# Weights ahead of tokens, statistics in pairs: a reordered start of a two-layer diffusion kernel

## The reference, cut to what matters

```python
shift, scale, gate = silu(c) @ ada_w[0] + ada_b[0]            # for latent tokens
c_shift, c_scale, c_gate = silu(c_ctx) @ ada_w[0] + ada_b[0]  # for context tokens
hx = rmsnorm(x, norm_w[0]) * (1 + scale) + shift
hc = rmsnorm(ctx, norm_w[0]) * (1 + c_scale) + c_shift
lb = softmax-cumsum of the lower-bound logits                 # tables for the gates
f  = lb + (1 - lb) * sigmoid(h @ w_f)                         # forward and backward gates
v, q, z = h @ w_v, silu(h @ w_q), silu(h @ w_z)
```

## Time and profile before

| what | value |
|---|---|
| median of 3 runs | 2157.39 us (2153.93 to 2157.52) |
| the profiled execution | 2153.69 us, with a span of 2151.9 us |
| TensorE busy | 2059.3 us, 96% |
| VectorE busy | 1304.1 us, 61% |
| ScalarE busy | 931.9 us, 43% |
| GpSimd busy | 476.2 us, 22% |
| moved by DMA | 144.45 MB, 67 GB/s over the span |

### The profile page before, as it was taken

The page is one execution under the profiler, slowest core; times in us unless marked ns, Lnnn a source line. Parts: engine busy times, 40 slices in busy tenths (PEclk is TensorE's granted clock), DMA queues, the critical chain, the costliest instruction groups (busy, mean ns, idle before and its releaser), DMA issues.

```text
span 2151.9 us, 30236 instructions
## 1 busy us (share of the span) xinstructions
PE 2059.3 (96%) x11372; PEld 1490.5 (69%) x11554; DVE 1304.1 (61%) x2360; ACT 931.9 (43%) x1960; POOL 476.2 (22%) x450
## 2 busy tenths in 40 slices
PE   5799999999999999999999999899999999999998
PEld 2567767767767767767767767677766666666665
DVE  7848648648648548548548548755563637465444
ACT  5746346346346346346356356344423131314222
POOL 2032222222222221221221222200161312100000
PEclk8899999999999999999999999999999999999999
DMA  7220110110110110110110110543321111204443
GB/s 278 79 69 11 45 55 11 45 54 11 45 54 11 46 53 11 47 53 11 54 45 11 60 40 1 186 147 122 123 71 50 45 51 33 88 10 148 147 147 117
DMA packets 106753, 144.45 MB, mean 67 GB/s; under 512 B 7136, under 2 KB 74224, under 8 KB 105584
## 3 DMA queue, kind: packets, MB, share of 16 engines
q1 hardware_dynamic: 99648, 125.72, 18.1%
q10 hardware_dynamic: 6960, 16.80, 2.0%
HBM read 108.91 MB, written 33.57 MB: 66 GB/s over the span
## 4 chain that ended last, share of the span: by engine, by line
PE 80%; ACT 7%; DVE 7%; issue 3%; DMA 2%; POOL 0%; SPq 0%; DVEq 0%; ACTq 0%; POOLq 0%
PE bank L1308 22%; PE bank L1309 21%; PE bank L1313 20%; PE bank L1464 4%; PE bank L1443 3%; PE bank L1475 3%; PE bank L1548 3%; PE bank L1450 2%; DVE xb L1074 2%; ACT xa L727 1%; ACT xa L729 1%; PE bank L1427 1%; ACT xb L737 1%; DVE xa L1038 1%; DMA ada_sb<-in_ada_w 1%
## 5 line engine op out<-in xcount | busy, mean ns | idle before, releaser
L1308 PE MATMUL bank<-h_hi,w_hi 128*128 128x512 f32 (+1 forms) x1472 | 576.6, 396 | 0.0
L1309 PE MATMUL bank<-h_hi,w_lo 128*128 128x512 f32 (+1 forms) x1472 | 550.6, 379 | 0.0
L1308 PEld LDWEIGHTS bank<-h_hi,w_hi 128*128 128x128 f32 x1472 | 279.3, 190 | 54.7
L1309 PEld LDWEIGHTS bank<-h_hi,w_lo 128*128 128x128 f32 x1472 | 279.3, 190 | 47.6
L1313 PE MATMUL bank<-h_lo,w_bf 128*128 128x512 bf16 (+1 forms) x1351 | 303.3, 365 | 7.9 <-issue 1.3
L1313 PEld LDWEIGHTS bank<-h_lo,w_bf 128*128 128x128 bf16 x1472 | 133.7, 98 | 142.7 <-issue 25.1
L1117 DVE SCALAR_TENSOR_TENSOR w_st<-w_st,cv,bank 128x128 f32<-128x128 f32 x560 | 194.2, 347 | 24.1 <-DVE w_st L1117 0.5
L1308 PE MATMUL bank<-wo_hi,og_hi 128*128 128x512 f32 x496 | 197.9, 399 | 3.1 <-DVE og_lo L1154 2.2
L1309 PE MATMUL bank<-wo_hi,og_lo 128*128 128x512 f32 x496 | 193.6, 390 | 0.0
L612 POOL TENSOR_TENSOR q<-qp,cv 128x512 f32<-128x512 f32 x64 | 71.9, 1124 | 524.9 <-PE bank L1443 244.1
L586 POOL TENSOR_TENSOR w_hi<-w_raw,zero_col 128x512 fp32r<-128x512 f32 x80 | 91.9, 1149 | 430.7 <-DMA w_raw<-in_w_in 228.7
(11 more groups left out here) (180 smaller groups left out, 3543.8 us busy)
## 6 DMA issues: line engine op xcount, KB each, us to landing
w_raw<-in_w_in SPq DMA_DIRECT2D x80, 256.0 KB, 2.8
ada_sb<-in_ada_w SPq DMA_DIRECT2D x8, 1024.0 KB, 13.9
xt<-in_x SPq DMA_DIRECT2D x16, 512.0 KB, 6.5
ada_a<-in_ada_late SPq DMA_DIRECT2D x64, 128.0 KB, 2.1
ada_b<-in_ada_late SPq DMA_DIRECT2D x64, 128.0 KB, 2.1
gated_scratch<-o_t ACTq DMA_DIRECT2D x32, 256.0 KB, 2.4
xr<-in_x SPq DMA_DIRECT2D x16, 512.0 KB, 5.0
x_scratch<-xr ACTq DMA_DIRECT2D x16, 512.0 KB, 2.6
```

Source lines behind the costliest of these rows:

```text
L1308: pe.matmul(out_ap, hi, m_hi, start=start, stop=False)
L1309: pe.matmul(out_ap, lo, m_hi, start=False, stop=False)
```

## The change

SyncE loads the eight pieces of `ada_w` ahead of the two context tiles. The statistics of the context tiles move behind the rounding of `ada_w`. Latent tiles are handled in pairs by `token_pair`: two sums of squares, then one logarithm and one exponential for both. Tiles 2 and 3 are done before the first modulate; the other pair of the group behind modulate 3 of the context group, and in later groups the pairs come behind modulates 2 and 5. VectorE scales a pair after the split that follows. The gate tables (`head_tables`) are made at step 3, ahead of the split of the last group, and `hv` and `hg` are copied there for head 0. GpSimd waits at step 0 until `hf_ready` is 32 (four groups split) before it cuts halves 2 and 3.

```diff
+        def pair_behind(g, k):
+            if g + 1 == len(GT0):
+                return None
+            return {3: GT0[1][0] + 2}.get(k) if g == 0 else {2: GT0[g + 1][0], 5: GT0[g + 1][0] + 2}.get(k)
+
+        def token_pair(act, t):
+            for i in (t, t + 1):
+                act.wait_ge(s[f"x_in{i % 8}"], 16 * (i // 8 + 1))
+                act.activation(junk0[:, :], xt0[:, i % 8, :], ACT.Square, accum_out=ssq[:, 0, i:i + 1]
+                               ).then_inc(s["nrm_act"], 1)
+                act.wait_ge(s["nrm_act"], 3 * t + i - t + 1)
+            act.activation(rstd[:, 0, t:t + 2], ssq[:, 0, t:t + 2], ACT.Ln, scale=1.0 / D,
+                           bias=eps[:, 0:1]).then_inc(s["nrm_act"], 2)
+            act.wait_ge(s["nrm_act"], 3 * t + 4)
+            act.activation(rstd[:, 0, t:t + 2], rstd[:, 0, t:t + 2], ACT.Exp, scale=-0.5
+                           ).then_inc(s["nrm_act"], 2)
+            rms_n[0] += 6
...
@@ modulate_first, ScalarE
-                if k % 2 and g + 1 < len(GT0):
-                    token_stats(act, GT0[g + 1][0] + k // 2)
+                if pair_behind(g, k) is not None:
+                    token_pair(act, pair_behind(g, k))
...
@@ SyncE
-            for t in range(2):
-                load_x0(sp, t)
             for k in range(KT):
                 sp.dma_start(ada_sb[:, k, :, :], ...)
+            for t in range(2):
+                load_x0(sp, t)
...
@@ GpSimd, head
+                    if first and st == 0:
+                        pool.wait_ge(s["hf_ready"], KT * (len(GT0) - 1))
                     for dh, m in CUTS.get(st, []):
...
@@ ScalarE
-            for t in range(2):
-                token_stats(act, t)
             (rounding of ada_w)
+            token_stats(act, 0)
             (copies of mrow, two exponentials for the tables)
+            token_stats(act, 1)
+            token_pair(act, 2)
             act.wait_ge(s["set_dve"], 5)
             modulate_first(act, 0)
...
@@ VectorE
-            for t in range(2):
-                normalise(t)
             (remainders of ada_w)
+            normalise(0)
             (copies of mrow)
-            (eleven instructions of the gate tables)
+            normalise(1)
             (gadd, gmul)
+            def head_tables():
+                (the same eleven instructions)
...
@@ split_first, VectorE
-                    if k % 2 and g + 1 < len(GT0):
-                        normalise(GT0[g + 1][0] + k // 2)
+                    if k and pair_behind(g, k - 1) is not None:
+                        for t in range(2):
+                            normalise(pair_behind(g, k - 1) + t)
+            for t in range(2, 4):
+                normalise(t)
             split_first(0)
...
@@ head, VectorE
+                if not first:
+                    head_vectors(h)
                 for st in range(NG):
+                    if first and st == NBLK - 1:
+                        head_tables()
+                        head_vectors(h)
                     if first and st < NBLK:
                         split_first(st + 1)
...
-                    if st == 2:
+                    if st == (NBLK - 1 if first else 2):
                         need(dve, "og_ready", NBLK, h, 0)
                         dve.tensor_copy(hg[:, :], head_tab[:, bass.ds(h, 1), 5]).then_inc(s["head_vec"], 1)
```

More of the change, by code:

```diff
@@ L934, in normalise @@
             def normalise(t):
-                dve.wait_ge(s["nrm_act"], 3 * (t + 1))
+                dve.wait_ge(s["nrm_act"], 3 * (t + 1 if t < 2 else t // 2 * 2 + 2))
                 dve.tensor_scalar(xt0[:, t % 8, :], xt0[:, t % 8, :], rstd[:, 0, t:t + 1], None,
                                   ALU.mult).then_inc(s["xn0"], 1)
-            for t in range(2):
-                normalise(t)
             for n in range(2 * KT):
@@ L969, in _ @@
                                          ALU.add, ALU.mult).then_inc(s["set_dve"], 1)
+            def head_tables():
+                dve.wait_ge(s["set_act"], 3)
+                step(dve.tensor_tensor(lbt[:, 4, :], lbt[:, 2, :], lbt[:, 3, :], ALU.add))
+                step(dve.reciprocal(lbt[:, 4, :], lbt[:, 4, :]))
+                step(dve.tensor_tensor(lbt[:, 0, :], lbt[:, 2, :], lbt[:, 4, :], ALU.mult))
+                for d in range(2):
+                    step(dve.tensor_copy(head_tab[:, :, 2 * d], lbt[:, 0, 8 * d:8 * d + 8]))
+                    step(dve.tensor_scalar(head_tab[:, :, 2 * d + 1], lbt[:, 0, 8 * d:8 * d + 8], -1.0, 1.0,
+                                           ALU.mult, ALU.add))
+                    step(dve.tensor_scalar(head_tab[:, :, 6 + d], lbt[:, 0, 8 * d:8 * d + 8], 1.0, None,
+                                           ALU.subtract))
+                step(dve.tensor_copy(head_tab[:, :, 5], vcol[:, R_GN:R_GN + 8]))
+                dve.tensor_copy(late[:, :], vcol[:, R_ADAB + 2 * KT:R_ADAB + 6 * KT]).then_inc(s["late_sum"], 1)
             def split_first(g):
@@ L982, in split_first, with head_vectors @@
                                       ).then_inc(s["hf_ready"], 1)
-                    if k % 2 and g + 1 < len(GT0):
-                        normalise(GT0[g + 1][0] + k // 2)
+                    if k and pair_behind(g, k - 1) is not None:
[3 more added lines that the diff above has]
+                normalise(t)
             split_first(0)
-            def head(h, first, last):
+            def head_vectors(h):
                 dve.tensor_copy(hv[:, :], head_tab[:, bass.ds(h, 1), :].rearrange("p a b -> p (a b)")
@@ L991, in head @@
                 need(dve, "head_vec", 2, h, 1)
+            def head(h, first, last):
+                if not first:
+                    head_vectors(h)
                 for st in range(NG):
+                    if first and st == NBLK - 1:
+                        head_tables()
+                        head_vectors(h)
                     if first and st < NBLK:
```

## The result

| | before | changed |
|---|---|---|
| median of 11 runs each, us | 2155.09 (2152.06 to 2157.91) | 2161.09 (2156.63 to 2163.46) |
| ratio, with its 95% interval | | 1.0025 [1.0016, 1.0034] |
| profiled execution: span, us | 2151.9 | 2160.1 |

The changed kernel is slower by 5.4 us (0.0025 x 2155.09); the interval of the ratio gives 3.4 to 7.3 us, and the two medians differ by 6.0. So the kernel did get slower; the 4.3 us that the prediction took for the least that can be told lie inside this interval. That figure started from 2157.39, a median of three; eleven executions of the kernel before give 2155.09.

A forecast was written before the change was run, and what follows sets the result against it. TensorE, busy from 108 us on in a fixed order, was taken to pass on any shift of the start almost unchanged. Terms -6.1 - 2.0 + 4.9 + 6.7 + 1.9 = +5.4 us on 2157.39 gave 2162.8 us, range 2153 to 2166.

The forecast's parts named there:

- opening: Start to first modulate: weights loaded first and tables off the path bring it to 36.7 from 42.83 us, -6.1 us.
- context group: From its first modulate to group 1's: one pair replaces four single statistics, 10.2 us instead of 12.15, -2.0 us.
- groups 1 to 3: Intervals between first modulates: pairs make ScalarE and VectorE wait in turn, 48.3 us instead of 43.4 for three, +4.9 us.
- tables beside cuts: Step 3, ahead of group 4's split: VectorE's table instructions are stretched by GpSimd's deferred cuts, +6.7 us.
- low clock: Last transposes of group 4: TensorE, idle before, runs at 1.2 GHz, transposes 1.77 us apart, +1.9 us.
- sum at the marker: Shift of the fifth group's last transpose, at 104.59 us before: all terms together, +5.4 us.
- from the marker to the third `k_tok`: Stretch from the fifth group's last transpose into head 0: the shift was to arrive almost unchanged, 0 us added.
- The rival in which ScalarE sets the pace: Groups 1 to 3: intervals shrink by 0.9 us, giving -2.7 instead of +4.9; total 2155.2 us; 16%.
- The rival in which they run side by side: Step 3: tables run beside GpSimd's cuts unstretched, costing 2.4 us, 4.3 less; total 2158.5 us; 14%.
- The rival of full clock: Groups 1 to 4: TensorE stays at full clock, groups cost 2.0 us and the clock nothing; total 2158.0 us; 20%.

The follow-up runs named there:

- cuts at 36: Changed kernel with one-tile statistics in groups 1 to 3, gate tables behind the last split, GpSimd's halves 2 and 3 cut from `hf_ready` 36; ratio to before 0.9964.
- single statistics: Changed kernel with statistics of groups 1 to 3 made one tile at a time behind every second modulate, as before; ratio to the kernel before 0.9988.
- the two experiments: Changed kernel with late tables and undeferred cuts, once with pairs kept (2151.75 us, one execution), once with one-tile statistics in groups 1 to 3 (ratio to before 0.9969).
- Cuts at once: Changed kernel without GpSimd's wait at step 0, so halves 2 and 3 are cut right behind the first slice; tables stay at step 3; 2155.99 us, one execution.
- tables after the split: Changed kernel with gate tables and `hg` moved to step 4, behind the last group's split; GpSimd's cuts stay deferred; 2160.29 us, one execution.
- cuts at 8 and 16: Changed kernel with one-tile statistics in groups 1 to 3, tables behind the last split, half 2 cut at `hf_ready` 8, half 3 at 16; ratio to before 0.9966.
- its best part alone: Changed kernel with one-tile statistics in groups 1 to 3, tables behind the last split, cuts not deferred; ratio to the kernel before 0.9969.

## Why the prediction was right, step by step

| step | predicted | first profiles | second profiles |
|---|---|---|---|
| opening | -6.1 | -7.1 | -5.8 |
| context group | -2.0 | -1.8 | -2.0 |
| groups 1 to 3 | +4.9 | +4.0 | +5.5 |
| tables beside cuts | +6.7 | +6.2 | +6.2 |
| low clock | +1.9 | +1.95 | +1.95 |
| sum at the marker | +5.4 | +3.15 | +5.8 |
| from the marker to the third `k_tok` | 0 | +1.7 | +0.8 |

Each column of profiles compares one execution of the changed kernel with one of the kernel before. The mean at the marker is +4.5, 0.9 below the forecast: the opening brought 0.4 more, and the tables cost 0.5 less. The step of the tables is the first split's distance behind its modulate, 6.96 us against 0.80.

**The opening** was a microsecond larger than I gave it in the first profile, and 0.3 smaller in the second. The mechanism stands: with the context tiles first, the first modulate moves by 4.5 us, and most of what isn't bytes is work that meets GpSimd. But I fixed this term too precisely. The changed kernel's second profile has its first modulate at 36.88, close to my 36.7, and cuts at 36, whose opening has no other edit, at 37.43 against 35.73 in single statistics. In these two TensorE was at a different clock between 32 and 34.5 us, first single statistics, then cuts at 36:

```profile
32.00:34.50 2.50, 2.50 (x20) 2.50 (x19) 0.89 (x1) 2.40 (x7) 2.50 (x3) 0.76 1.04 411
```

```profile
32.00:34.50 2.50, 2.50 (x14) 2.50 (x13) 0.86 (x1) 2.40 (x7) 2.50 (x3) 0.50 1.05 413
```

Where the clock is 0.50, the turning of `mrow` into columns ends later (`gadd` starts at 34.61 in the changed kernel's first profile and at 35.80 in its second), and the rest with it. A term on which an opening's waits and clock bear has a spread of 1 to 2 us.

**The pairs.** That two engines that took turns with overlap now wait for each other was right, and the idle 2.35 us of VectorE under a pair show it. The size was right too. The three intervals took 16.1, 16.0 and 15.3 us in the first profile, the last with the full clock at its start, for which I had 15.2; and 15.5, 16.5 and 16.1 in the second, against my 15.6, 16.3 and 16.3. Over all the runs, three intervals with pairs take 46.3 to 48.1 us (six profiles), and 41.2 to 43.4 with single statistics and no cuts beside them (five, with the two of before). The 3.9 us that the two experiments give lie at the low end of this. The rival in which ScalarE sets the pace is out: intervals would have been under 14.5.

**Tables beside cuts.** Six of twelve instructions ended with one of GpSimd's six, as worked out. "Cuts at once" and "tables after the split" take away one of the two each, and in both the stretch behind group 4's first modulate shrinks (8.64 and 10.74 us, not 14.28). The rival in which they run side by side is out; 2.4 us, its price, is what the tables take alone. The step came out 0.5 us below its 6.7: GpSimd's six took 5.6 us from start to end, where I had 5.9, and with the reciprocal passing only five small instructions were left behind them.

The Trainium skill's rule ("SBUF — State Buffer", sections "Summary: rules for kernel authors" and "Who interferes with whom") holds here: VectorE and GpSimd share a port pair as an exclusive lock, and its list of the VectorE instructions that ask for it has no reciprocal. The trace agrees with both. The reciprocal took 0.25 us at 94.94 beside GpSimd's `w_bf`, and 0.25 alone in "cuts at once".

**The clock.** The size was right to a tenth, and the experiment that keeps the clock up shows it to be the clock and not the pace of VectorE. The rival of full clock is out for the changed kernel. At this step it holds in "single statistics", though, where TensorE waited 2.83 us and not 5.97. The length of the last wait alone doesn't decide it: the clock was 0.50 behind a wait of 1.77 us in "tables after the split" (102 to 106 us), and low behind one of 2.76 in "cuts at once" (0.70 between 94 and 98). So the terms don't add up when one is taken away. Undoing the pairs gave 8.1 us at the marker: 3.9 ahead of group 4's first modulate, 2.3 because the tables were done sooner behind it (4.7 us, not 7.0), and 1.9 of clock.

**What failed** is the sentence that behind the marker TensorE waits for nothing and the shift arrives unchanged. In head 0 it waits for ScalarE's `k_tok`, for 3.2 and 3.1 us in the two profiles of the changed kernel and for 1.5 and 3.1 in those of before, and falls to a low clock in both kernels. From the second to the third copy of `k_tok` it took 8.46 and 8.52 us in the changed kernel, 6.67 and 7.27 in that of before. That the total matched +5.4 to the tenth is luck: the mean at the marker was 0.9 short, 1.3 was added behind it, which the prediction had put at nothing, and the ratio's own interval is 3.4 to 7.3 us. The direction and the terms ahead of the marker are not luck. Whether the 1.3 us belong to the change is open. From the marker to the third `k_tok` the two profiles of before took 68.7 and 69.9 us and the two of the changed kernel 70.5 and 70.7, but "cuts at 8 and 16" and "cuts at 36", which have none of its three costly edits, took 70.2 and 70.9. In the kernel before a stretch at low clock fell at another place:

```profile
153.00:156.00 3.00, 3.00 (x9) 2.35 (x8) 1.92 (x2) 1.77 (x5) 0.00 (x0) 0.51 0.00 0
```

So what arrives of a shift at the start is the shift within one or two microseconds, as these waits and stretches of low clock happen to fall.

## What to carry to other kernels

A new order has to be read on both engines that hand work to each other: a pair of small jobs is cheaper on its own engine, and dearer if it opens a gap on the other. Work deferred from a crowded stretch needs a destination without long or chained instructions of an engine that it excludes; here the start gained 9 us up to group 1, and the place to which tables and cuts went gave back 8 of it, 2 of them by the low clock, and the pairs another 4 to 5. Undo the parts of a mixed change one by one: here its best part alone was 6.7 us faster than the kernel before, and the whole was 5.4 slower. Compare such parts over a stretch that repeats between executions, and not only at one instant: here two markers 4.2 us apart held 1.8 us of chance.

## What the runs showed of the hardware that was not expected

- A chain of small instructions beside GpSimd advances by one instruction for each of GpSimd's, apart from the reciprocal, which passes: twelve took 6.1 us, and 2.4 alone. It works both ways: GpSimd's `w_lo`, 1.26 us alone, took 1.71 (tables after the split) and 1.74 (cuts at 36) beside VectorE's splits, and a split's cast 1.49 in place of 0.43.
- The same program's opening differs by 1.2 us between two executions (first modulate at 35.69 and 36.88), with TensorE granted 0.75 and 0.50 of its clock between 32 and 34.5 us. Two programs whose openings have the same instructions differ by 1.7 (35.73 and 37.43).
- 36 transposes of an identity in a wait of 6 us (4.09 us of work, then 2.06 idle) left the granted clock at 1.00, where it had been 0.50 behind 5.97 us of idleness.
